# Two-block transformer layer on one core: 16 pairs of the gated up projection as Strassen products

## The reference

```python
def conv_ffn(h, w_up, conv_w, conv_b, w_down):      # h: 512 x 1024, normalised
    u = h @ w_up                                     # 1024 -> 2 * 2816
    u = causal depthwise conv of width 3 over tokens (u, conv_w) + conv_b
    gate, val = jnp.split(u, 2, axis=-1)
    return (jax.nn.silu(gate) * val) @ w_down        # 2816 -> 1024
x = x + conv_ffn(rms_norm_2(x, norm_ffn), w_up, conv_w, conv_b, w_down)
return rms_norm_2(x, norm_final)
```

## Time and profile before

| | us |
|---|---|
| median of the three runs | 1575.79 |
| the profiled execution, its own time | 1575.11 |
| its span, first to last instruction | 1573.3 |
| outside its span (1575.11 - 1573.3) | 1.8 |

### The profile page before, as it was taken

How to read it: one execution, slowest core, us unless ns; L and a number is a source line. 1 busy time by engine, 2 the same in 40 slices (tenths; PEclk the granted TensorE clock), 3 DMA queues, 4 the chain that set the end, 5 groups by cost and what they waited for, 6 DMA issues and landing times. The chain is left out here.

```text
span 1573.3 us, 23154 instructions
## 1 busy us (share of the span) xinstructions
PE 1557.0 (99%) x8050; PEld 1275.6 (81%) x8050; DVE 819.7 (52%) x1531; ACT 740.9 (47%) x1269; POOL 844.5 (54%) x974
## 2 busy tenths in 40 slices
PE   9999999999999999999999999999999999999997
PEld 6677776777888899999987887779988888888886
DVE  5496986664235645444445446553334551552454
ACT  6435786554325544444444435553744432342342
POOL 6444664333555677666655542266554655556553
PEclk9999999999999999999999999999999999999999
DMA  5322232213232233333333421133322333233231
GB/s 187 109 92 69 81 94 68 63 58 117 96 96 94 81 96 106 108 107 108 96 121 105 118 71 55 55 119 121 109 80 94 94 94 107 84 103 107 80 107 67
DMA packets 46153, 150.18 MB, mean 95 GB/s; under 512 B 4648, under 2 KB 9904, under 8 KB 46064
## 3 DMA queue, kind: packets, MB, share of 16 engines
q1 hardware_dynamic: 39648, 140.00, 28.4%
q10 hardware_dynamic: 6416, 8.98, 1.8%
HBM read 146.73 MB, written 2.11 MB: 95 GB/s over the span
## 5 line engine op out<-in xcount | busy, mean ns | idle before, releaser
L447 POOL TENSOR_TENSOR w_lo<-w_raw,w_hi 128x256 fp32r<-128x256 f32 x800 | 621.6, 811 | 593.2 <-ACT w_hi L1317 593.1
L1317 ACT ACTIVATE w_hi<-w_raw 128x1024 fp32r<-128x1024 f32 x200 | 207.5, 1050 | 197.8 <-PE job L530 186.6
L528 PE MATMUL job<-a_hi,w_hi 128*128 128x512 f32 (+1 forms) x730 | 282.6, 387 | 1.4 <-POOL w_lo L447 0.7
L530 PE MATMUL job<-a_hi,w_lo 128*128 128x512 f32 (+1 forms) x730 | 277.6, 380 | 0.0
L529 PE MATMUL job<-a_lo,w_hi 128*128 128x512 f32 (+1 forms) x730 | 277.4, 380 | 0.0
L528 PE MATMUL job<-b_hi,w_hi 128*128 128x512 f32 x680 | 269.5, 396 | 0.8 <-DVE sq L1981 0.5
L530 PE MATMUL job<-b_hi,w_lo 128*128 128x512 f32 x680 | 265.0, 390 | 0.0
L529 PE MATMUL job<-b_lo,w_hi 128*128 128x512 f32 x680 | 264.7, 389 | 0.0
L453 POOL TENSOR_TENSOR w_lo<-w_raw,w_hi 128x512 fp32r<-128x512 f32 x114 | 148.1, 1305 | 110.1 <-ACT w_hi L1586 107.4
L528 PEld LDWEIGHTS job<-a_hi,w_hi 128*128 128x128 f32 x730 | 137.2, 188 | 45.9 <-issue 13.2
L530 PEld LDWEIGHTS job<-a_hi,w_lo 128*128 128x128 f32 x730 | 137.3, 188 | 26.4
(11 more groups left out here) (414 smaller groups left out, 2765.4 us busy)
## 6 DMA issues: line engine op xcount, KB each, us to landing
w_raw<-w_all SPq DMA_DIRECT2D x264, 512.0 KB, 3.5
arena<-x_t ACTq DMA_DIRECT2D x8, 512.0 KB, 6.3
out_t<-arena SPq DMA_DIRECT2D x6, 256.0 KB, 2.2
arena<-rg_w ACTq DMA_DIRECT2D x1, 1024.0 KB, 7.8
arena<-mem_t ACTq DMA_DIRECT2D x1, 1024.0 KB, 7.2
spare<-row_table ACTq DMA_DIRECT2D x3, 256.0 KB, 4.5
arena<-consts ACTq DMA_DIRECT2D x1, 512.0 KB, 3.9
out_t<-arena ACTq DMA_DIRECT2D x2, 256.0 KB, 2.2
```

The lines of the kernel that those rows point to most:

```text
L447: nc.gpsimd.tensor_tensor(w_lo[:, sl, c], raw[:, sl, c], w_hi[:, sl, c].bitcast(F32), ALU.subtract).then_inc(s("lo_ready"), 1)
L528: mm(ps[:, 0:n], w_hi[:, sl, c], hi[:, kt, 0:n], start=kt == 0, stop=False)
L530: ins = mm(ps[:, 0:n], w_lo[:, sl, c], hi[:, kt, 0:n], start=False, stop=kt == last)
L1317: fn(w_hi[:, sl], raw[:, sl], ACT.Copy).then_inc(s("hi_ready"), 1)
```

## The change

It redoes 16 of the 22 pairs of up jobs, pairs 5 to 20, as seven products each, with the existing helpers `ff_p1` to `ff_p7`; pairs 0 to 4 and 21 stay plain. Each of these 16 blocks also has two down half jobs, one behind T1 and one behind T3 ("apart"). The down product of the hidden tiles 0 to 15 moves into the blocks (32 half jobs of 12 matmuls), that of the last six stays as eight jobs at the end, with six input tiles each. `f_c` moves from SBUF to the PSUM banks `t_ps[1]` and `o_ps`, `f_h` to `o_ps` as well, `f_silu` to `spare`. The sums S1 to S4 are made during the plain pairs 0 to 3, between a pair's take and its filter. The loops become written-out code. The weights are laid out anew; their number of tiles stays.

```diff
+GLU_PAIRS = 22
+GLU_PLAIN = (0, 1, 2, 3, 4, 21)
+GLU_BLOCKS = range(FF_PAIRS + 5, FF_PAIRS + 21)
+def glu_units():
+
+    order = [tag for p in range(5) for tag in glu_jobs(p)]
+    for n in GLU_BLOCKS:
+        d = ff_downs(n)
+        order += [("W21", n), ("W11", n), ("T1", n), d[0], ("T2", n), ("W22", n), ("T3", n), d[1], ("T4", n)]
+    return order + glu_jobs(GLU_PAIRS - 1)
...
+        f_c = [t_ps[1], o_ps]
+        f_h = o_ps
...
@@ TensorE @@
-                with pe.Fori(1 if gi == 0 else 0, g // 2) as i:
-                    for c in range(4):
-                        job(k + c, b_hi, b_lo, m=i)
...
+            for p in range(1, 5):
+                for u in range(2):
+                    pe.wait_ge(s("ff_part"), FF_PART["act", FF_PAIRS + p - 1, u])
+                    glu_plain(p, u)
+            for n in GLU_BLOCKS:
+                d = ff_downs(n)
+                ff_p2(n)
+                ff_p1(n)
+                ff_p5(n)
+                glu_down(d[0])
+                ff_p6(n)
+                ff_p3(n)
+                ff_p7(n)
+                glu_down(d[1])
+                ff_p4(n)
+            pe.wait_ge(s("ff_part"), FF_PART["C11", GLU_BLOCKS[-1]])
+            glu_plain(GLU_PAIRS - 1, 0)
+            pe.wait_ge(s("ff_part"), FF_PART["C12", GLU_BLOCKS[-1]])
+            glu_plain(GLU_PAIRS - 1, 1)
...
@@ GpSimd @@
+            for n in GLU_BLOCKS:
+                first_sums(n)
+                d = ff_downs(n)
+                ff_low("W21", n)
+                ff_low("W11", n)
+                ff_low(*d[0])
+                ff_sum("T3", n, ff_block("W22", n), ff_block("W12", n))
+                ff_sum("T4", n, ff_block("W21", n), ff_source(("T2", n)), ALU.add)
+                ff_low("W22", n)
+                ff_low(*d[1])
...
@@ ScalarE @@
+            def conv_head2(p, u):
+
+                act.wait_ge(s("ff_part"), FF_PART["act", FF_PAIRS + p, u])
+                if u == 1 and p > 0:
+                    act.wait_ge(s("hlo_ready"), p)
+                fn(f_c[u][:], f_u[u][:, PAD:PAD + T], ACT.Identity, scale=vcol("conv_w2", 88 + 22 * u + p),
+                   bias=vcol("conv_b2", 22 * u + p)).then_inc(s("f_head"), 1)
...
+            for p in range(5):
+                if p < 4:
+                    high_jobs(p + 1, 1)
...
+                if p < 4:
+                    upper(4 + p)
+                conv_head2(p, 0)
+                if p < 4:
+                    s_high(4 + p)
...
+                conv_head2(p, 1)
+                silu(p)
+                hidden_high(p)
+            ff_high("T3", GLU_BLOCKS[0])
+            for n in GLU_BLOCKS:
...
+                if n > GLU_BLOCKS[0]:
+                    conv_head2(p - 1, 0)
+                ff_high(*d[1])
+                ff_high("T4", n)
+                copy_u1(n)
+                if n > GLU_BLOCKS[0]:
+                    silu(p - 1)
+                ff_high(*(("W21", nxt) if more else last[0]))
+                copy_p5(n)
+                ff_high(*(("W11", nxt) if more else last[1]))
+                if n > GLU_BLOCKS[0]:
+                    hidden_high(p - 1)
+                ff_high(*(("T1", nxt) if more else last[2]))
+                copy_u2(n)
+                if more:
+                    ff_high(*ff_downs(nxt)[0])
+                    ff_high("T2", nxt)
+                    ff_high("W22", nxt)
...
+                conv_head2(p, 1)
+                if more:
+                    ff_high("T3", nxt)
...
@@ VectorE @@
+            def glu_c21(n):
+
+                dve.wait_ge(s("ff_used"), FF_USED["T4", n])
+                tt(f_u[0][:, PAD + 256:PAD + T], ff_c1, rstd[:, 256:T], ALU.mult).then_inc(s("ff_part"), 1)
...
+            for p in range(5):
+                glu_take(p, 0)
+                if p < 4:
+                    half_sums(4 + p)
+                glu_conv(p, 0)
+                if p < 4:
+                    half_rests(4 + p)
+                glu_take(p, 1)
+                glu_conv(p, 1)
+                if p == 4:
+                    sum_low("T1", GLU_BLOCKS[0])
+                glu_product(p)
+                if p == 4:
+                    sum_low("T2", GLU_BLOCKS[0])
+                glu_low(p)
+            dve.wait_ge(s("ff_copied"), FF_COPY["rstd", 1])
+            for n in GLU_BLOCKS:
...
+                if not first:
+                    glu_c21(n - 1)
+                sum_low("T3", n)
+                if not first:
+                    glu_conv(p - 1, 0)
+                c11(n)
+                glu_c11(n)
+                if not first:
+                    glu_product(p - 1)
+                sum_low("T4", n)
+                if not first:
+                    glu_low(p - 1)
+                down_add(d[0])
+                if more:
+                    sum_low("T1", nxt)
+                c12(n)
+                if more:
+                    sum_low("T2", nxt)
+                c22(n)
+                glu_second(n)
+                glu_conv(p, 1)
+                down_add(d[1])
```

More of the change, by code:

```diff
@@ L92, in ff_units, with glu_jobs @@
     return order + [("D", 7, d) for d in range(8)]
-FF_ORDER = ff_units()
+def glu_jobs(p):
+    return [("job", ff_job(FF_PAIRS + p) + u, half) for u in range(2) for half in range(2)]
+def glu_units():
[4 more added lines that the diff above has]
+    return order + glu_jobs(GLU_PAIRS - 1)
+FF_STAGE = len(ff_units())
+FF_ORDER = ff_units() + glu_units()
 FF_UNIT = {tag: u for u, tag in enumerate(FF_ORDER) if tag}
@@ L1235, in _ @@
                 job(J_OC + c, a_hi, a_lo)
[L1237 to L1244, removed]
-                with pe.Fori(1 if gi == 0 else 0, g // 2) as i:
-                    for c in range(4):
-                        job(k + c, b_hi, b_lo, m=i)
[L1248 to L1261, removed]
-                    job(k + c, a_hi, a_lo, last=g - 1)
-                k += 8
@@ new lines, in _ @@
+            pe.wait_ge(s("job_taken"), J_FF2 - 1)
+            for half in range(2):
+                tag = ("job", FF_JOBS, half)
+                ff_wait(tag)
+                for kt in range(4 * half, 4 * half + 4):
+                    pe.wait_ge(s("xlo_ready"), 32 + kt + 1)
+                    ins = ff_half(tag, [kt], job_ps[0], b_hi, b_lo, 0, 7)
+                ins.then_inc(s("ff_used"), 1)
+            norm_all(4)
+            pe.wait_ge(s("job_taken"), J_FF2)
+            glu_plain(0, 1)
@@ new lines, in _ @@
+            pe.wait_ge(s("ff_added"), 64 + 32)
+            block_of(k + 1, range(4), a_hi, a_lo, last=TAIL - 1)
+            for kt in (4, 5):
+                pe.wait_ge(s("hlo_ready"), h0 + kt + 1)
+                ins = block_of(k, [kt], a_hi, a_lo, last=TAIL - 1)
+            ins.then_inc(s("job_done"), 1)
+            block_of(k + 1, range(4, 6), a_hi, a_lo, last=TAIL - 1).then_inc(s("job_done"), 1)
+            for c in range(2, 7):
+                job(k + c, a_hi, a_lo, last=TAIL - 1)
@@ new lines, in _ @@
+            p = GLU_PAIRS - 1
+            conv_head2(p - 1, 0)
+            split(J_FF2 + 1)
+            silu(p - 1)
+            hidden_high(p - 1)
+            conv_head2(p, 0)
+            split(J_FF2 + 2)
+            conv_head2(p, 1)
+            silu(p)
+            hidden_high(p)
+            for f in range(8):
+                if J_FF2 + 3 + f < J_END:
+                    split(J_FF2 + 3 + f)
+                if f < 7:
+                    act.wait_ge(s("job_taken"), J_FF2 + f + 1)
+                    square_tile(5, f, x[:, f, :])
@@ new lines, in glu_conv, with glu_product @@
+            def glu_conv(p, u):
+                dve.wait_ge(s("f_head"), GLU_CONV[p, u])
+                for j in range(2):
+                    ins = stt(f_c[u][:], f_u[u][:, PAD - 2 + j:PAD - 2 + j + T],
+                              vcol("conv_w2", 44 * j + 22 * u + p), f_c[u][:], ALU.mult, ALU.add)
+                    if j == 0:
+                        did(ins)
+                        settle()
+                ins.then_inc(s("f_conv"), 1)
+            def glu_product(p):
+                dve.wait_ge(s("f_silu"), p + 1)
+                dve.wait_ge(s("f_conv"), 2 * p + 2)
+                tt(f_h[:], f_silu, f_c[1][:], ALU.mult).then_inc(s("f_prod"), 1)
@@ new lines, in glu_low @@
+            def glu_low(p):
+                dve.wait_ge(s("hhi_ready"), p + 1)
+                dve.wait_ge(s("f_prod"), p + 1)
+                tt(a_lo[:, p % 8, :], f_h[:], a_hi[:, p % 8, :].bitcast(F32), ALU.subtract).then_inc(
+                    s("hlo_ready"), 1)
+            for p in range(5):
+                glu_take(p, 0)
[12 more added lines that the diff above has]
+                glu_low(p)
@@ L2734, in last_inverse @@
+            p = GLU_PAIRS - 1
+            glu_c21(GLU_BLOCKS[-1])
+            glu_conv(p - 1, 0)
+            glu_product(p - 1)
+            glu_low(p - 1)
+            glu_take(p, 0)
+            glu_conv(p, 0)
+            glu_take(p, 1)
+            glu_conv(p, 1)
+            glu_product(p)
+            glu_low(p)
+            for f in range(7):
```

(2 more changed lines are left out.)

360 lines of the change are left out of this document (218 added, 142 removed).

## The result

The changed kernel takes **1563.83 us** (median of four runs, 1563.61 to 1564.22) against 1576.03 (1575.38 to 1576.68) for the kernel before: 12.2 us less, ratio 0.9923 (95% interval 0.9906 to 0.9940). The forecast was 1566.4, range 1563 to 1573. The profiled execution took 1563.86 us, 1562.0 of them its span.

The account below looks back on a forecast made before the run. TensorE's stream was taken to bound the stage end to end. From 1575.1, 11.9 us of saved matmul time and 2.5 lost at the seam gave 1565.7, hence a median of 1566.4 us, range 1563 to 1573.

Parts of the forecast that it names:

- TensorE's work: In the 16 redone pairs, 84 matmuls of 256 columns replace 48 of 512: 0.74 saved per pair, -11.9 us.
- Blocks without waits: In the new blocks TensorE never waits: cost 0, with margin 0.6 us on the chain from T3 to W11.
- The banks: Filters and product in PSUM keep VectorE free of the SBUF port lock, so the stt pair takes 1.54, not 2.14.
- Rival 3: Slower: W11 waits for C21 1.1 us a block if banks don't free the stt pair: +17.6, 1584; chance 0.07.
- Plain pairs, 0: Pairs 0 to 4 keep 10.88 us though VectorE gets the sums: 0, bounds 0 and 1.5.
- The seam: From pair 4 to the first block, T1 waits for VectorE's low part: +2.5 us once, bounds 1.3 and 4.5.
- End of the stage: Pair 21's chain into the last eight jobs, their loads, norm and stores stay as before: 0.
- The sum: Whole kernel: 1575.1 - 11.9 + 2.5 = 1565.7 for the profiled execution; its 0.7 below the median makes 1566.4.
- rival 1: At the seam from pair 4 to the first block there is no cost: 1563.9; chance 0.07.
- Rival 2: Each block waits 0.1 to 0.55 us, T2's low part being late: +1.6 to +8.8, 1568 to 1575; chance 0.20.
- Rival 4: In the blocks only columns count, so a pair saves 1.36: 1556.5 with the seam; chance 0.04.

Follow-up runs that it names:

- experiment 9: Changed kernel with product T1 of all 30 blocks as 24 matmuls of 128 columns in place of 12 of 256: 1602.79 us, ratio 1.0171.
- experiment 6: Changed kernel with two more VectorE steps per block between the last filter and the second down half's add: 1570.78 us.
- experiment 4: Changed kernel with filters and product put back from PSUM banks into SBUF tiles: 1596.74 us, ratio 1.0133 against the kernel before.
- experiment 5: Changed kernel with only the product of SiLU and filter put back in SBUF, filters left in PSUM banks: 1564.18 us.
- experiment 3: Changed kernel with VectorE's low parts of T1 and T2 and several ScalarE copies and high parts moved earlier at the first new block: 1562.79 us.
- 7: Changed kernel with both down halves of a block together behind T1 instead of apart: 1587.87 us, ratio 1.0075 against the kernel before.
- 8: Changed kernel with four matmuls of product W22 left out in each of the 16 new blocks, output less exact: 1556.10 us.

## Why the prediction was right, and where it was off

- **TensorE's work, -11.9:** right. Predicted 15.58 a block, measured 15.57; the plain pairs ahead of the seam take 55.30 us, before's pace. The rule of the Trainium skill ("TensorE: Matmul & The Clock Gate", Part 1) by which only 2.5 ns stand beside the columns would have given 19.0; the measured pitches, 0.2267 and 0.12, go against it. But my reading of them, "a fixed part of about 0.013 us", holds between 256 and 512 columns only (experiment 9).
- **Blocks without waits, 0:** right, and for the reason given. The room was predicted at 0.6 and measured at 0.8 (experiment 6). VectorE was put at 12.4, GpSimd at 11.7 and ScalarE at 9.8 us a block; they were 12.8, 12.3 and 8.9. VectorE's low parts of sums were taken at a mean of 0.94 us, from the quieter earlier blocks, and had 1.16. The stt pair in banks was taken at 1.54 and took 1.55.
- **The banks:** the step on which most hung. Rival 3 had the right place and both of its terms, and for filters and product in SBUF too low a price: 1.88 us a block, not 1.1, from 1.17 for the stt pair (0.6 taken) and 1.43 for the late c22 (1.1 taken), less a room of 0.8 (experiment 4). The lock that the Trainium skill states ("SBUF - State Buffer") agrees with the rows of experiment 5: the step with two SBUF inputs pays, the one with an operand in a bank doesn't.
- **Plain pairs, 0:** right.
- **The seam, +2.5: the step that was mis-sized.** Measured 1.6. The place and the releaser were right. VectorE's loop per plain pair was taken at 10.75 us, with ScalarE's `upper` late in each. It came late once, by 0.64, and the four loops took 10.50, 10.96, 10.44 and 10.45 (takes from 1211.49 to 1253.84). So at the last take VectorE was 0.4 us behind TensorE (1256.82, where 1256.45 was possible) and not 1.4 as in the sum, and T1's low part ended at 1260.50 instead of 1261.8. The slip is the lower bound from the data's own chain, 1.3, and that lag.
- **End of the stage, 0:** off by 0.55 us in the change's favour, by the two pairs of profiles, and by 0.2 more from the norm to the end (13.3 against 13.1). Cause open.
- **The sum.** Own time 1563.86 against 1565.7: 1.84 less than forecast, of which the seam is 0.85 to 0.9, the stage's end 0.7 and its earlier start 0.3, which may be chance. The 0.7 added for the low profiled execution of before did not come on top: the changed kernel's profiled execution was at its median. That 0.7 was not looked into: the kernel before has executions with and without the fall of the clock in its last half job, 1575.95 and 1575.11 in the two profiles.
- **Rivals.** The time is rival 1's to 0.1 us, but its mechanism (no cost at the seam) isn't what happened; experiment 3 comes nearest to it, with 0.48 left. It is thanks to rival 1 that the range reaches down to the measured time at all; the agreement is luck. Rival 2 was wrong, since the room held. Rival 4 was wrong, since the pitch stayed 0.12.

## What to carry to other kernels

When a tuned stage is one engine's stream, price a change by that engine's pitch, then name the tightest chain between two uses of a bank and its room: here both came out within 0.2 us a block, and a delay costs only what exceeds the room. A change that removes matmul time can live on where a tile lies: with filters and product in SBUF the same change loses 21 us. At the seam between two patterns the late steps stand in a queue over several engines, and removing the first of them gave back 0.6 of 1.65 us. Below 256 columns, narrower matmuls gain next to nothing where each loads its own weights. And before a small difference is put down to a change, the granted clock of both stretches is to be read: here each of its falls cost 1.2 to 1.7 us.

## What the runs showed of the hardware that was not expected

- A matmul of this type costs 0.2267 us at 512 columns, 0.12 at 256 and 0.11 at 128. At 256 the kernel stands next to a floor, which is the pace of the weight loads: the one matmul of 128 columns whose weights are there already is followed after 0.06.
- A VectorE step of 512 columns with two SBUF inputs has a mean of 1774 ns at a place of the block where GpSimd is at work, where 0.69 is its time undisturbed; the pair of stt reached 2.72 in place of 1.55. The rows of before, from quieter stretches, gave a mean of 938 and 2.14.
- Behind the seam's wait the granted clock fell to 0.50 for 3.4 us in three profiles: experiment 4 (T1 4.5 us late), 7 (2.6) and 9 (1.6). In four others with a slip of 1.6 (both of the changed kernel, experiments 6 and 8) it stayed at 1.00. Each fall cost 1.6 to 1.7 us, so a wait of 1.6 cost twice as much in one of five profiles.
- One and the same step of the last norm starts 0.37 us later in one program than in the other, in both profiles of each.
